# Roots moved from GpSimd to VectorE, and the links of the norm chains spread over more slots

## The chip, the cores and the metric

The kernel runs on one core of one Trainium2 chip. The number that counts is the device time of one execution in microseconds, as a median over runs. Before the change it is 1972.41 us (three runs, 1971.65 to 1972.62).

## What is computed

Two transformer blocks on 256 tokens of width 2048, in fp32, with weights read once from HBM. Cut to what matters here:

```python
# block 1
h = rms_norm(x, norm1_g);  proj = h @ w_in          # 2048 x 6160
qb = rms_norm(qb.reshape(B, S, 8, 128), q_norm_g)   # queries and keys, a norm a head
kb = rms_norm(kb.reshape(B, S, 8, 128), k_norm_g)
out_a = gla_mixer(...)                              # its heads end in rms_norm(o) * silu(r)
out_b = dilated_mixer(qb, kb, vb, rel_bias)
x = x + concat(out_a, out_b) @ w_out
h2 = rms_norm(x, norm2_g)
x = x + (silu(h2 @ w_gate) * (h2 @ w_up)) @ w_down
# block 2, even layer: retention (heads end in rms_norm_nogain(o) * silu(g)) beside a convolution
x = x + even_mixer(rms_norm_2(x, ev_norm_w), ...)
# block 2, odd layer: 32 query heads and 4 key heads of 64
q, k, v, gate = split(rms_norm_2(x, od_norm_w) @ w_in)
q = rope(rms_norm_2(q.reshape(b, s, 32, 64), q_norm_w), pos)
k = rope(rms_norm_2(k.reshape(b, s, 4, 64), k_norm_w), pos)
x = x + (swa_sinks(q, k, v, sinks) * silu(gate)) @ w_out
```

Each `rms_norm` needs one reciprocal square root a row and head: a "root".

## The kernel before

**Products.** Every large product is cut into blocks of 512 output columns, and each block into units of two 128-row slices of weights (eight units where the sum is over 2048). A weight tile comes by DMA into `raw`; ScalarE rounds it to `wh` and VectorE writes the rest, `wl = raw - wh`. This pair is called a cut. A unit on TensorE (`mul`) is then 12 matmuls of 128x512: `wh*xh`, `wl*xh`, `wh*xl` for two slices and two halves of the tokens. There are three buffers of `wh` and `wl` (`NS`), so the cut of unit u+2 waits until unit u-1 is done, and is made while unit u runs.

**The order.** `Plan.lay` writes one list, `plan.order`, and every engine walks the same list and issues its own part of each entry, strictly in that order. For each unit u it says `cut u+2`, then `mul u` first half, then one `step`, then `mul u` second half. A `step` lets each of three lanes (`att`, `fin`, `post`) go on to its next `yield`. So a lane has one slot a unit, in the middle of it. When a block's last unit is said, `launch("post", after(b))` first drains the lane (runs what is left of the former block's work at once, without a slot between), and then says the first entry of the new one. Each norm chain of the queries and keys lives in `post`, and the blocks it runs beside are of eight units, so it has eight slots before it is drained.

**A chain.** For queries and keys of block 1: `qk_evac` (ScalarE, PSUM to `W0`, which is the first half of `TW`, and the square into `W1`, the second half), `qk_sum` (VectorE), the root, `qk_norm` (VectorE multiplies `W0`), and two `qk_turn` (TensorE transposes, ScalarE copies out). The odd layer has `ok_evac` or `oq_evac`, `on_sum`, the root, `on_norm`, `on_rope` twice (six VectorE operations each; the second waits for the first), for the keys also `ok_dup` (four copies), then two turns, which wait for the last `on_rope` (of the keys, for `ok_dup`).

**The root before.** GpSimd runs `root`: 14 small operations on a tile of 128 x 2, 8 or 16 (`st`), each waiting for the one before. Between the first and the second VectorE does one shift, `halve`, which follows its sum at once and waits until GpSimd has made the mean. The same list entry (`qk_sum`, `on_sum`, `g_sum`, `r_sum`, `norm`) holds the sum, the shift and the root. Entries that use the result (`qk_norm`, `on_norm`, `g_n`, `r_n`, and `evacuate` by `rr` for `norm`) wait for `s_root`. There are 21 roots: four of the residual stream, four of block 1's queries and keys, four of GLA heads, four of retention heads, five of the odd layer.

**Other places.** The heads of the odd layer run in lane `att`; `afin` (VectorE, three operations) finishes four of them, and `mix M5` (TensorE transposes of `AW`) follows in lane `fin` after two yields. After the last half of an output block, `add` (VectorE) adds it to `x`, `sq` (ScalarE) squares it for the next norm, and two `xturn` (TensorE transposes of `x`) make the next activations.

Of the kernel before, what the change touches and what calls it, by code (L numbers as in the profile page):

```python
# [7 lines left out]
S, D = 256, 2048  # L8
# [104 lines left out]
class Plan:  # L113
# [78 lines left out]
    def after(self, b):  # L192
        say, kind, a = self.say, b.done[0], b.done[1:]
        if kind == "add":
# [3 lines left out]
            if final and stage < 4:  # L198
                say("sq", stage, j)
                yield  # L200
                for h in range(2):
                    say("xturn", f"X{stage}", 4 * j + 2 * h)
                    yield
                if j == 3:
                    say("norm", stage)
            elif final:
                say("out", j)
        elif kind == "qk":
            key, j = a
# [66 lines left out]
        elif kind == "cg":  # L276
            j = a[0]
            say("cg", j, b.i)
            yield
            yield  # L280
            for h in range(2):
                say("cg_turn", j, h)
                yield
                say("cmix", "M4", 8 + 4 * j + 2 * h, j, h)
                yield
        elif kind == "okv":
            say("ok_evac", b.i)
            yield
            yield from self.od_norm("k")
            say("ok_dup")  # L290
            yield
            yield
            for k in range(2):
                say("ok_turn", k)
                yield
        elif kind == "oq":
            say("oq_evac", a[0], b.i)
            yield
            yield from self.od_norm(a[0])
            yield  # L300
            yield
            for k in range(2):
                say("oq_turn", a[0], k)
                yield
        else:
            assert kind == "og"
            say("og", a[0], b.i)
            yield
            self.lanes["att"].append(self.od_heads(a[0]))

    def od_norm(self, x):
        self.say("on_sum", x)
        yield
        yield
        self.say("on_norm", x)
        yield
        self.say("on_rope", x, 0)
        yield
        self.say("on_rope", x, 1)
# [48 lines left out]
    def finish(self, a, g):  # L368
        self.say("afin", a, g)
        yield  # L370
        yield
        if a == "d":
            self.say("mix", "M0", 8 + 2 * g, "d", g)
        else:
            self.say("mix", "M5", 2 * g, "o", g)
        yield

    def gla(self):
# [24 lines left out]
        for n in range(6):  # L403
# [4 lines left out]
            if n >= 2:  # L408
                say("g_n", n - 2)
# [6 lines left out]
    def retention(self):  # L416
        say = self.say
        for h in range(4):
# [6 lines left out]
            yield  # L425
            yield
# [31 lines left out]
def program(nc, t, out):  # L458
# [50 lines left out]
    for p in plan.order:  # L509
# [9 lines left out]
        if p[0] in ("g_o", "r_pv"):  # L519
# [3 lines left out]
                                            ("norm", "qk_sum", "g_sum", "r_sum", "on_sum"))}  # L523
# [7 lines left out]
    with ctx:  # L531
# [41 lines left out]
        s_root_v, s_root_y, s_root = sem("s_root_v"), sem("s_root_y"), sem("s_root")  # L573
# [405 lines left out]
        def scalar(e):  # L979
# [16 lines left out]
            for p in plan.order:  # L996
# [48 lines left out]
                elif kind == "qk_evac":  # L1045
# [8 lines left out]
                    on.wait_ge(*taken(b))  # L1054
# [128 lines left out]
                elif kind in ("ok_evac", "oq_evac"):  # L1183
# [3 lines left out]
                    if kind == "ok_evac":  # L1187
                        on.wait_ge(s_cg, 2)
                        width = 256
                    else:  # L1190
                        on.wait_ge(s_dup, 2)
                        if a[0]:
                            on.wait_ge(*full("oq_turn", a[0] - 1, 1))
                        width = 512
                    evacuate(T3, b)
                    on.wait_ge(*taken(b))
                    on.wait_ge(s_rope, ropes[("eq_rope", "k", 1, 1)] if kind == "ok_evac" else
                               ropes[("on_rope", a[0] - 1 if a[0] else "k", 1)])
# [20 lines left out]
        def vector(e):  # L1219
# [16 lines left out]
            def halve(p, n):  # L1236

                on.wait_ge(s_root_v, roots[p])
                ts1(ry_[:, 0:n].bitcast(i32), rv_[:, 0:n].bitcast(i32), 1,
                    ALU.logical_shift_right).then_inc(s_root_y, 1)  # L1240

            for p in plan.order:
# [25 lines left out]
                elif kind == "norm":  # L1268
# [4 lines left out]
                    halve(p, 2)  # L1273
# [8 lines left out]
                elif kind == "qk_sum":  # L1282
# [5 lines left out]
                    halve(p, 8)  # L1288
                elif kind == "qk_norm":
                    v = W0.rearrange("p (g d) -> p g d", d=128)  # L1290
                    on.wait_ge(s_root, roots[("qk_sum",) + a])
# [141 lines left out]
                elif kind == "g_sum":  # L1433
# [4 lines left out]
                    halve(p, 2)  # L1438
                elif kind == "g_n":
                    m = a[0]  # L1440
                    k, h2 = gparts[m]
                    on.wait_ge(s_root, roots[("g_sum", m)])
# [45 lines left out]
                elif kind == "r_sum":  # L1488
# [5 lines left out]
                    halve(p, 2)  # L1494
                elif kind == "r_n":
                    h = a[0]
                    on.wait_ge(s_root, roots[("r_sum", h)])
# [47 lines left out]
                elif kind == "on_sum":  # L1545
# [9 lines left out]
                    halve(p, 2 * n)  # L1555
                elif kind == "on_norm":
                    n = 4 if a[0] == "k" else 8
                    on.wait_ge(s_root, roots[("on_sum",) + a])
# [14 lines left out]
        def gpsimd(e):  # L1573
            on = Once(e)
            steps = Steps(s_pool_step)
            done = (s_root, 0)

            def root(p, dst, src, n, width, from_, dst_free=()):

                v, y, q = rv_[:, 0:n], ry_[:, 0:n], rq_[:, 0:n]  # L1580
                yi = y.bitcast(i32)
                on.wait_ge(*from_)
                if roots[p] > 1:
                    on.wait_ge(s_root, roots[p] - 1)
                e.tensor_scalar(v, src, 1.0 / width, 1e-6, ALU.mult, ALU.add).then_inc(s_root_v, 1)  # L1585
                on.wait_ge(s_root_y, roots[p])
                on.wait_ge(*steps.mark(e.tensor_scalar(yi, yi, -1.0, 1597463007.0, ALU.mult, ALU.add)))
                for i in range(3):
                    on.wait_ge(*steps.mark(e.tensor_tensor(q, y, y, ALU.mult)))  # L1589
                    on.wait_ge(*steps.mark(e.tensor_tensor(q, q, v, ALU.mult)))  # L1590
                    on.wait_ge(*steps.mark(e.tensor_scalar(q, q, -0.5, 1.5, ALU.mult, ALU.add)))
                    if i < 2:
                        on.wait_ge(*steps.mark(e.tensor_tensor(y, q, y, ALU.mult)))
                for sem_n in dst_free:
                    on.wait_ge(*sem_n)
                e.tensor_tensor(dst, q, y, ALU.mult).then_inc(s_root, 1)

            for p in plan.order:
                kind, a = p[0], p[1:]
                if kind == "norm":  # L1600
                    free = []
                    if a[0]:
                        was = [taken(b.i) for b in blocks if b.acts == f"X{a[0] - 1}"]
                        for s in (s_read_act, s_read_dve):
                            n = [v for z, v in was if z is s]
                            if n:
                                free.append((s, max(n)))
                    if a[0] == 1:
                        free.append(full(*find("gates")))
                    root(p, rr, nsum, 2, D, (s_nsum, a[0] + 1), free)  # L1610
                elif kind == "qk_sum":
                    root(p, rs[:, 0:8], rs[:, 0:8], 8, 128, (s_qk_sum, nth(*p)))
                elif kind == "g_sum":
                    root(p, rg[a[0]], rg[a[0]], 2, 256, (s_g_sum, nth(*p)))
                elif kind == "r_sum":
                    root(p, rsa, rsa, 2, 256, (s_r_sum, nth(*p)))
                elif kind == "on_sum":
                    n = 8 if a[0] == "k" else 16
                    root(p, rs[:, 0:n], rs[:, 0:n], n, 64, (s_on_sum, nth(*p)))
                elif kind == "bias":  # L1620
# [158 lines left out]
```

## Time and profile before

| | |
|---|---|
| profiled execution | 1971.09 us, span 1969.3 us, granted TensorE clock 1.00 |
| median of the runs | 1972.41 us |
| TensorE busy | 1946.4 us of the span (99%), 9062 matmuls |
| VectorE, ScalarE, GpSimd busy | 1095.9, 939.1, 108.5 us |
| DMA | 178 GB/s read from HBM over the span |

TensorE is busy nearly all the time, and matmuls overlap: a 128x512 matmul is shown as 0.39 us long while the next starts 0.23 us after it. So a wait of TensorE reads some 0.16 us shorter in the list of waits than the time it costs between two starts. What another engine does matters only where TensorE waits for it.

### The profile page before, as it was taken

How to read it: one execution, taken by the hardware profiler on the slowest of the kernel's cores; microseconds unless marked ns; L12 is line 12 of the kernel's file. 1: busy time of each engine (PE TensorE's matmuls, PEld its weight loads, DVE VectorE, ACT ScalarE, POOL GpSimd, SP SyncE). 2: the span in 40 equal slices, each digit the busy share in tenths (PEclk: the TensorE clock that was granted, in tenths of full speed). 3: DMA queues.
4: the chain of work that ended last, by engine and by line, in shares of the span. 5: the costliest groups of instructions: out<-in, count | busy, mean ns of one | idle time of the engine just before them, and what ended most of it. 6: DMA issues, size and time to landing. Idle time of an engine off the chain costs nothing.

```text
span 1969.3 us, 22692 instructions
## 1 busy us (share of the span) xinstructions
PE 1946.4 (99%) x9062; PEld 1600.0 (81%) x9062; DVE 1095.9 (56%) x1330; ACT 939.1 (48%) x1230; POOL 108.5 (6%) x326
## 2 busy tenths in 40 slices
PE   8999999999999999999999999999999999999998
PEld 6788887788888888888888888888888888787787
DVE  4556455664545545445445556544655665666674
ACT  6445354554444344443444554444444464655653
POOL 1111000200000000000000010001100003001100
PEclk9999999999999999999999999999999999999999
DMA  7566564466665666665666566665566655544445
GB/s 238 175 193 171 152 173 159 154 179 192 186 192 190 193 193 190 187 189 193 193 190 191 182 193 183 192 193 171 168 184 189 192 179 176 150 150 141 138 149 161
DMA packets 182441, 352.74 MB, mean 179 GB/s; under 512 B 11136, under 2 KB 11952, under 8 KB 182336
## 3 DMA queue, kind: packets, MB, share of 16 engines
q1 hardware_dynamic: 181520, 349.18, 58.3%
q0 software_dynamic: 816, 2.11, 0.7%
q8 instruction: 71, 1.16, 0.2%
q14 instruction: 34, 0.28, 0.0%
HBM read 349.14 MB, written 2.11 MB: 178 GB/s over the span
## 4 chain that ended last, share of the span: by engine, by line
PE 93%; DVE 3%; POOL 1%; ACT 1%; issue 1%; DMA 0%; DVEq 0%; SPq 0%; ACTq 0%
PE g L790 29%; PE g L792 29%; PE g L791 29%; PE m L755 3%; DVE wl L1225 1%; ACT TW L985 1%; DVE st L1234 1%; PE m L871 1%; DVE TW L1225 1%; ACT wh L988 0%; POOL st L1589 0%; PE ob L889 0%; PE ob L888 0%; PE ob L887 0%; PE m L862 0%
## 5 line engine op out<-in xcount | busy, mean ns | idle before, releaser
L1225 DVE TENSOR_TENSOR wl<-raw,wh 128x1024 fp32r<-128x1024 f32 x657 | 801.5, 1222 | 770.7 <-ACT wh L988 770.1
L988 ACT ACTIVATE wh<-raw 128x1024 fp32r<-128x1024 f32 x657 | 694.5, 1058 | 837.6 <-PE g L792 834.9
L790 PE MATMUL g<-wh,xh 128*128 128x512 f32 x1888 | 748.0, 396 | 2.7 <-DVE wl L1225 2.7
L792 PE MATMUL g<-wh,xl 128*128 128x512 f32 x1888 | 736.8, 390 | 0.0
L791 PE MATMUL g<-wl,xh 128*128 128x512 f32 x1888 | 735.7, 390 | 0.0
L790 PEld LDWEIGHTS g<-wh,xh 128*128 128x128 f32 x1888 | 354.8, 188 | 80.1 <-issue 5.5
L792 PEld LDWEIGHTS g<-wh,xl 128*128 128x128 f32 x1888 | 354.6, 188 | 75.2
L791 PEld LDWEIGHTS g<-wl,xh 128*128 128x128 f32 x1888 | 355.1, 188 | 70.4
L790 PE MATMUL g<-wh,mh 128*128 128x512 f32 x736 | 291.5, 396 | 0.0
L792 PE MATMUL g<-wh,ml 128*128 128x512 f32 x736 | 287.1, 390 | 0.0
L791 PE MATMUL g<-wl,mh 128*128 128x512 f32 x736 | 286.7, 390 | 0.0
L790 PEld LDWEIGHTS g<-wh,mh 128*128 128x128 f32 x736 | 138.2, 188 | 31.2 <-issue 3.9
L792 PEld LDWEIGHTS g<-wh,ml 128*128 128x128 f32 x736 | 138.1, 188 | 29.4
L791 PEld LDWEIGHTS g<-wl,mh 128*128 128x128 f32 x736 | 138.3, 188 | 27.3
L1585 POOL TENSOR_SCALAR st<-st 128x2 f32<-128x2 f32 (+2 forms) x21 | 4.1, 194 | 1632.0 <-DVE st L1234 1631.7
L1225 DVE TENSOR_TENSOR x<-g,x 128x512 f32<-128x512 f32 x72 | 46.4, 685 | 20.0 <-PE g L792 20.0
L985 ACT ACTIVATE A<-g,st 128x512 f32<-128x512 f32 x50 | 31.7, 684 | 31.5 <-PE g L792 31.5
L1091 ACT ACTIVATE PB<-PB,st 128x128 f32<-128x128 f32 x80 | 35.6, 446 | 8.4 <-DVE st L1231 8.4
L988 ACT ACTIVATE xh<-m,small 128x256 fp32r<-128x256 f32 x64 | 26.8, 470 | 20.0 <-PE m L755 20.0
L1228 DVE SCALAR_TENSOR_TENSOR xl<-m,small,xh 128x256 fp32r<-128x256 f32 x64 | 28.0, 479 | 14.4 <-ACT xh L988 14.4
L988 ACT ACTIVATE mh<-m 128x512 fp32r<-128x512 f32 x38 | 22.7, 597 | 26.9 <-PE m L755 26.9
L985 ACT ACTIVATE TW<-g,st 128x512 f32<-128x512 f32 x34 | 21.5, 684 | 24.0 <-PE g L792 19.2
(131 smaller groups left out, 840.4 us busy)
## 6 DMA issues: line engine op xcount, KB each, us to landing
raw<-in_ev_w_in SPq DMA_DIRECT2D x128, 512.0 KB, 3.7
raw<-in_w_in SPq DMA_DIRECT2D x96, 512.0 KB, 3.9
raw<-in_w_gate SPq DMA_DIRECT2D x88, 512.0 KB, 4.3
raw<-in_w_up SPq DMA_DIRECT2D x88, 512.0 KB, 3.7
raw<-in_w_down SPq DMA_DIRECT2D x88, 512.0 KB, 4.7
raw<-in_od_w_in SPq DMA_DIRECT2D x72, 512.0 KB, 3.6
raw<-in_w_out SPq DMA_DIRECT2D x32, 512.0 KB, 4.3
raw<-in_ev_w_out SPq DMA_DIRECT2D x32, 512.0 KB, 3.7
```

The source lines that it names most:

```text
L755: last = e.transpose(dst(c), src(c), ident)
L790: e.matmul(o, hi[:, kt, c], h, start=first, stop=False)
L791: e.matmul(o, hi[:, kt, c], l, start=False, stop=False)
L792: last = e.matmul(o, lo[:, kt, c], h, start=False, stop=end)
L871: last = e.transpose(o[:, 128 * c:128 * c + 128], L[:, 128 * c:128 * c + 128], ident)
L985: return e.activation(o, i, func, scale=scale, bias=bias)
L988: return e.activation(o, i, AF.Copy, scale=scale)
L1091: last = e.activation(L[:, lo:hi], L[:, lo:hi], AF.Exp, bias=mx[:, h, kb:kb + 1], accum_out=sm[:, h, kb:kb + 1])
L1225: return e.tensor_tensor(o, a, b, op)
L1228: return e.scalar_tensor_tensor(out=o, in0=a, scalar=s, in1=b, op0=op0, op1=op1)
L1234: return e.tensor_reduce(o, i, AX, op, negate=negate)
L1585: e.tensor_scalar(v, src, 1.0 / width, 1e-6, ALU.mult, ALU.add).then_inc(s_root_v, 1)
```

## The change

All of `root` moves to VectorE. The helper `halve` and GpSimd's `root` are gone; the root is 12 VectorE operations, and an entry of the list by itself (`qk_root`, `on_root`, `g_root`, `r_root`; for `norm` it stays in the entry). The square of a chain becomes an entry too (`qk_sq`, `on_sq`). The generators say the links with two yields between them instead of one or two. `mix M5` comes two yields later, `sq` goes behind the two `xturn` instead of ahead of them, and `norm` two yields later.

```diff
             if final and stage < 4:
-                say("sq", stage, j)
-                yield
                 for h in range(2):
                     say("xturn", f"X{stage}", 4 * j + 2 * h)
                     yield
+                say("sq", stage, j)
                 if j == 3:
+                    yield
+                    yield
                     say("norm", stage)
...
             say("qk_evac", key, j, b.i)
-            yield
-            say("qk_sum", key, j)
-            yield
-            yield
-            say("qk_norm", key, j)
-            yield
+            for p in ("qk_sq", "qk_sum", "qk_root", "qk_norm"):
+                yield
+                yield
+                say(p, key, j)
             yield
             for k in range(2):
                 say("qk_turn", key, j, k)
...
     def od_norm(self, x):
-        self.say("on_sum", x)
-        yield
-        yield
-        self.say("on_norm", x)
-        yield
-        self.say("on_rope", x, 0)
-        yield
-        self.say("on_rope", x, 1)
+        for p in ("on_sq", "on_sum", "on_root", "on_norm"):
+            yield
+            yield
+            self.say(p, x)
+        for k in range(2):
+            yield
+            self.say("on_rope", x, k)
...
         else:
+            yield
+            yield
             self.say("mix", "M5", 2 * g, "o", g)
...
+            def root(dst, src, n, width, from_, dst_free=()):
+                v, y, q = rv_[:, 0:n], ry_[:, 0:n], rq_[:, 0:n]
+                yi = y.bitcast(i32)
+                on.wait_ge(*from_)
+                on.wait_ge(*steps.mark(e.tensor_scalar(v, src, 1.0 / width, 1e-6, ALU.mult, ALU.add)))
+                on.wait_ge(*steps.mark(ts1(yi, v.bitcast(i32), 1, ALU.logical_shift_right)))
+                on.wait_ge(*steps.mark(e.tensor_scalar(yi, yi, -1.0, 1597463007.0, ALU.mult, ALU.add)))
+                for i in range(3):
+                    on.wait_ge(*steps.mark(stt(q, v, -0.5, y, ALU.mult, ALU.mult)))
+                    on.wait_ge(*steps.mark(tt(q, q, y, ALU.mult)))
+                    if i < 2:
+                        on.wait_ge(*steps.mark(stt(y, q, 1.5, y, ALU.add, ALU.mult)))
+                for sem_n in dst_free:
+                    on.wait_ge(*sem_n)
+                stt(dst, q, 1.5, y, ALU.add, ALU.mult).then_inc(s_root, 1)
```

Three places of the order, before and then after. In these rows `TW<-TW,st` is the norm's product, `TW<-TW,A` and the `TW<-TW` behind it are one `on_rope`, `wl<-raw,wh` is VectorE's part of a cut, and `st<-st` are the small operations of a root.

VectorE, from the sum to the last rope of the odd layer's first queries, before:

```order
L1234 TENSOR_REDUCE st<-TW 128x16
L1231 TENSOR_SCALAR st<-st 128x16
L1225 TENSOR_TENSOR wl<-raw,wh 128x1024 x2
L1225 TENSOR_TENSOR TW<-TW,st 128x512 x2
L1225 TENSOR_TENSOR wl<-raw,wh 128x1024
L1225 TENSOR_TENSOR TW<-TW,A 128x256 x4
L1225 TENSOR_TENSOR TW<-TW 128x8x32 x2
L1225 TENSOR_TENSOR wl<-raw,wh 128x1024
L1225 TENSOR_TENSOR TW<-TW,A 128x256 x4
L1225 TENSOR_TENSOR TW<-TW 128x8x32 x2
```

and after, from the root's last operation on:

```order
L1237 SCALAR_TENSOR_TENSOR st<-st 128x16
L1234 TENSOR_TENSOR wl<-raw,wh 128x1024 x2
L1234 TENSOR_TENSOR TW<-TW,st 128x512 x2
L1234 TENSOR_TENSOR TW<-TW,A 128x256 x4
L1234 TENSOR_TENSOR TW<-TW 128x8x32 x2
L1234 TENSOR_TENSOR TW<-TW,A 128x256 x4
L1234 TENSOR_TENSOR TW<-TW 128x8x32 x2
L1234 TENSOR_TENSOR wl<-raw,wh 128x1024 x3
```

The norm and the two ropes, which had a cut between each, now follow each other with none, and the norm has moved from the third of the block's eight slots to the last. In the list the norm stands in the middle of the block's last unit, and the ropes, the turns and the next evacuation directly behind that unit.

VectorE, where the GLA heads end (`A<-AW,st,A` and `A<-A,st` are `g_n`, `st<-A` is `g_sum`), before:

```order
L1225 TENSOR_TENSOR wl<-raw,wh 128x1024
L1234 TENSOR_REDUCE st<-A 128x2
L1231 TENSOR_SCALAR st<-st 128x2
L1228 SCALAR_TENSOR_TENSOR A<-AW,st,A 128x256 x2
L1225 TENSOR_TENSOR wl<-raw,wh 128x1024
L1234 TENSOR_REDUCE st<-A 128x2
L1231 TENSOR_SCALAR st<-st 128x2
L1228 SCALAR_TENSOR_TENSOR A<-A,st 128x256 x2
```

and after, one cut to the next:

```order
L1234 TENSOR_TENSOR wl<-raw,wh 128x1024
L1243 TENSOR_REDUCE st<-A 128x2
L1250 TENSOR_SCALAR st<-st 128x2
L1240 TENSOR_SCALAR st<-st 128x2
L1252 TENSOR_SCALAR st<-st 128x2
L1237 SCALAR_TENSOR_TENSOR st<-st 128x2
L1234 TENSOR_TENSOR st<-st 128x2
L1237 SCALAR_TENSOR_TENSOR st<-st 128x2 x2
L1234 TENSOR_TENSOR st<-st 128x2
L1237 SCALAR_TENSOR_TENSOR st<-st 128x2 x2
L1234 TENSOR_TENSOR st<-st 128x2
L1237 SCALAR_TENSOR_TENSOR st<-st 128x2
```

Where one shift stood, twelve operations stand between two cuts, and four such roots come in four slots that follow each other.

VectorE, behind an output block of block 1 (`x<-g,x` is `add`, `xl<-m,small,xh` the low half of an `xturn`), before:

```order
L1225 TENSOR_TENSOR x<-g,x 128x512 x2
L1225 TENSOR_TENSOR wl<-raw,wh 128x1024 x2
L1228 SCALAR_TENSOR_TENSOR xl<-m,small,xh 128x256 x2
L1225 TENSOR_TENSOR wl<-raw,wh 128x1024
L1228 SCALAR_TENSOR_TENSOR xl<-m,small,xh 128x256 x2
```

and after:

```order
L1234 TENSOR_TENSOR x<-g,x 128x512 x2
L1234 TENSOR_TENSOR wl<-raw,wh 128x1024
L1237 SCALAR_TENSOR_TENSOR xl<-m,small,xh 128x256 x2
L1234 TENSOR_TENSOR wl<-raw,wh 128x1024
L1237 SCALAR_TENSOR_TENSOR xl<-m,small,xh 128x256 x2
```

The first turn of `x` now stands one slot, that is one unit, nearer to the `add` it reads: half a unit of products behind it instead of one and a half.

## Rows read from the trace of the kernel before

**Rows 1.** Waits of TensorE: us in total, times, longest.

```profile
PE m L755 <- DVE AW L1225: 5.0, 3, 1.7
PE m L755 <- DVE TW L1225: 3.8, 5, 1.1
PE g L790 <- DVE wl L1225: 2.7, 4, 1.1
```

**Rows 2.** Timeline of an undisturbed unit: start us, us, engine, line, operation [idle before].

```profile
58.61 0.39 PE L790 MATMUL g<-wh,xh 128*128 128x512 f32 x1
...
58.87 1.06 ACT L988 ACTIVATE wh<-raw 128x1024 fp32r<-128x1024 f32 x1 [1.66 <-PE g L792]
...
59.96 1.23 DVE L1225 TENSOR_TENSOR wl<-raw,wh 128x1024 fp32r<-128x1024 f32 x1 [1.50 <-ACT wh L988]
...
61.33 0.39 PE L790 MATMUL g<-wh,xh 128*128 128x512 f32 x1
```

**Rows 3.** Timeline where the first root of the residual stream is awaited.

```profile
37.88 1.26 ACT L985 ACTIVATE TW<-g,st 128x512 f32<-128x512 f32 x2 [4.43 <-POOL st L1596]
...
42.50 0.50 PE L790 MATMUL g<-wh,xh 128*128 128x512 f32 x1 [1.09 <-DVE wl L1225]
```

**Rows 4.** Timeline of the first queries of block 1, norm and turn.

```profile
49.54 1.22 DVE L1225 TENSOR_TENSOR TW<-TW,st 128x1024 f32<-128x1024 f32 x1 [3.21 <-POOL st L1596]
...
50.82 0.66 PE L755 MATMUL m<-small,TW 128*128 128x128 f32 x4 [1.15 <-DVE TW L1225]
```

**Rows 5.** Timeline of the odd layer's first queries: norm, first rope, turn.

```profile
1671.23 1.29 DVE L1225 TENSOR_TENSOR TW<-TW,st 128x512 f32<-128x512 f32 x2 [3.38 <-POOL st L1596]
...
1673.58 1.42 DVE L1225 TENSOR_TENSOR TW<-TW,A 128x256 f32<-128x256 f32 x4
1675.03 0.76 DVE L1225 TENSOR_TENSOR TW<-TW 128x256 f32<-128x256 f32 x2
...
1679.12 0.65 PE L755 MATMUL m<-small,TW 128*128 128x128 f32 x4 [0.47 <-DVE TW L1225]
```

**Rows 6.** Timeline of finished heads, first of three such places.

```profile
1722.24 0.68 DVE L1225 TENSOR_TENSOR AW<-ob,st 128x512 f32<-128x512 f32 x1
...
1723.77 0.66 PE L755 MATMUL m<-small,AW 128*128 128x128 f32 x4 [1.66 <-DVE AW L1225]
```

**Rows 7.** Timeline of the odd layer's keys: norm, first rope, copies.

```profile
1647.44 0.76 DVE L1225 TENSOR_TENSOR TW<-TW,st 128x256 f32<-128x256 f32 x2 [2.92 <-POOL st L1596]
...
1649.25 0.89 DVE L1225 TENSOR_TENSOR TW<-TW,A 128x128 f32<-128x128 f32 x4
1650.17 0.49 DVE L1225 TENSOR_TENSOR TW<-TW 128x128 f32<-128x128 f32 x2
...
1653.17 0.90 DVE L1569 COPY A<-TW 128x256 f32<-128x256 f32 x4
```

**Rows 8.** Small operations of VectorE, by shape: busy us, mean ns | idle before.

```profile
L1231 DVE TENSOR_SCALAR st<-st 128x2 f32<-128x2 f32 x32 | 7.3, 229 | 1.1
...
L1225 DVE TENSOR_TENSOR st<-st 128x8 f32<-128x8 f32 x8 | 1.3, 164 | 0.0
```

**Rows 9.** Timeline behind an output block: next unit's first matmul, and the add.

```profile
375.44 0.39 PE L790 MATMUL g<-wh,mh 128*128 128x512 f32 x1
375.64 1.29 DVE L1225 TENSOR_TENSOR x<-g,x 128x512 f32<-128x512 f32 x2 [0.34 <-PE g L792]
```

**Rows 10.** Timeline of VectorE where the last GLA heads end.

```profile
357.02 0.68 DVE L1234 TENSOR_REDUCE st<-A 128x2 f32<-128x512 f32 x1
...
358.73 0.88 DVE L1228 SCALAR_TENSOR_TENSOR A<-A,st 128x256 f32<-128x256 f32 x2
```

**Rows 11.** Two matmuls near the start (timeline), and a window of the end.

```profile
10.20 0.63 PE L790 MATMUL g<-wh,xh 128*128 128x512 f32 x1
10.63 0.63 PE L791 MATMUL g<-wl,xh 128*128 128x512 f32 x1
...
1964.00:1969.00 5.00, 0.17 (x1) 0.00 (x0) 1.29 (x2) 0.00 (x0) 0.00 (x0) 0.84 0.30 105
```

More of the change, by code:

```diff
@@ L402, in gla @@
             yield
-        for n in range(6):
+        for n in range(7):
             if n < 4:
@@ L407, in gla @@
                 say("g_sum", n - 1)
-            if n >= 2:
-                say("g_n", n - 2)
+            if 2 <= n < 6:
+                say("g_root", n - 2)
+            if n >= 3:
+                say("g_n", n - 3)
             yield
@@ L425, in retention @@
             yield
+            say("r_root", h)
             yield
@@ L1053, in scalar @@
                     evacuate(T3, b)
-                    on.wait_ge(*taken(b))
+                elif kind == "qk_sq":
+                    key, j = a
+                    n = nth(*p)
+                    on.wait_ge(*taken(find("qk_evac", key, j)[-1]))
                     if n > 1:
@@ L1272, in vector @@
                     reduce(nsum, ss, ALU.add).then_inc(s_nsum, 1)
-                    halve(p, 2)
+                    free = []
+                    if a[0]:
+                        was = [taken(b.i) for b in blocks if b.acts == f"X{a[0] - 1}"]
+                        for s in (s_read_act, s_read_dve):
+                            n = [v for z, v in was if z is s]
+                            if n:
+                                free.append((s, max(n)))
+                    if a[0] == 1:
+                        free.append(full(*find("gates")))
+                    root(rr, nsum, 2, D, (s_nsum, a[0] + 1), free)
                 elif kind == "add":
@@ L1287, in vector @@
                     reduce(rs[:, 0:8], W1.rearrange("p (g d) -> p g d", d=128), ALU.add).then_inc(s_qk_sum, 1)
-                    halve(p, 8)
+                elif kind == "qk_root":
+                    root(rs[:, 0:8], rs[:, 0:8], 8, 128, (s_qk_sum, nth(*p)))
                 elif kind == "qk_norm":
                     v = W0.rearrange("p (g d) -> p g d", d=128)
-                    on.wait_ge(s_root, roots[("qk_sum",) + a])
+                    on.wait_ge(s_root, roots[("qk_root",) + a])
                     tt(v, v, rs[:, 0:8].unsqueeze(2).to_broadcast([128, 8, 128]), ALU.mult).then_inc(s_qk_norm, 1)
@@ L1437, in vector @@
                            ALU.add).then_inc(s_g_sum, 1)
-                    halve(p, 2)
+                elif kind == "g_root":
+                    m = a[0]
+                    root(rg[m], rg[m], 2, 256, (s_g_sum, m + 1))
                 elif kind == "g_n":
@@ L1441, in vector @@
                     k, h2 = gparts[m]
[L1442 removed]
+                    on.wait_ge(s_root, roots[("g_root", m)])
                     on.wait_ge(*taken(bi[("sr", 1)]))
@@ L1493, in vector @@
                     reduce(rsa, AW[:, 512:1024].rearrange("p (g d) -> p g d", d=256), ALU.add).then_inc(s_r_sum, 1)
-                    halve(p, 2)
+                elif kind == "r_root":
+                    root(rsa, rsa, 2, 256, (s_r_sum, a[0] + 1))
                 elif kind == "r_n":
                     h = a[0]
-                    on.wait_ge(s_root, roots[("r_sum", h)])
+                    on.wait_ge(s_root, roots[("r_root", h)])
                     on.wait_ge(*taken(bi[("gret", 1)]))
@@ L1554, in vector @@
                            ALU.add).then_inc(s_on_sum, 1)
-                    halve(p, 2 * n)
+                elif kind == "on_root":
+                    n = 8 if a[0] == "k" else 16
+                    root(rs[:, 0:n], rs[:, 0:n], n, 64, (s_on_sum, nth(*p)))
                 elif kind == "on_norm":
                     n = 4 if a[0] == "k" else 8
-                    on.wait_ge(s_root, roots[("on_sum",) + a])
+                    on.wait_ge(s_root, roots[("on_root",) + a])
                     norm_n = []
@@ L1575, in gpsimd @@
             steps = Steps(s_pool_step)
[L1576 to L1596, printed above, removed]
@@ L1598, in gpsimd @@
             for p in plan.order:
                 kind, a = p[0], p[1:]
[L1600 to L1620, printed above, removed]
+                if kind == "bias":
```

27 lines of the change are left out of this document (13 added, 14 removed).

## The prediction
> **What bounds the kernel now.** First the busy times: TensorE is the only engine near its limit, so a change of time must be a change in its work or its waits. Its work stays: the same products and transposes. So I read the list of its waits next [rows 1]: 5.0 us in three waits for finished heads (`AW`), 3.8 us in five for a chain's product (`TW`), 2.7 us in four for a cut. Each costs 0.16 us more than listed, since a matmul is shown 0.39 us long and the next starts after 0.23. The chain of waits behind each then shows the root: `qk_norm` and `on_norm` wait on VectorE for GpSimd's last operation for 3 us and more [rows 4, 5, 7], and cuts queue behind the waiting instruction.
>
> The measure for all that follows is an undisturbed unit [rows 2]. TensorE starts it at 58.61 and the next at 61.33: 2.72 us. ScalarE starts the cut for two units later at 58.87, because that is when the unit before is done, and VectorE's `wl` runs from 59.96 to 61.19, that is 1.35 to 2.58 us after the unit's start. What stands behind this `wl` on VectorE starts 2.5 us after the unit's start, however long VectorE was idle before. And `wl` is wanted 5.44 us after it: 2.85 us of cover.
>
> **What goes.** TensorE's stalls at the chains, counted between starts. The cut behind the first root: the evacuation waits on ScalarE 4.43 us for GpSimd, the cut behind it is late [rows 3]; a root on VectorE ends some 2 us sooner, so the 1.09+0.16 = 1.25 us go. Block 1's four chains: one wait of 1.15 [rows 4] and, of the same list, three of 0.72 (3.8 less 1.15 and 0.47, by three); with 0.16 each 3.9 us. The odd layer's first queries: 0.47 for the turn [rows 5] and two late cuts that make up, with 1.09 here and 0.63 at the start, the 2.7 of the list, so 0.97; with three times 0.16 1.9 us. The heads: 5.0+0.48 = 5.5 us; `afin` needs 1.4 us from 1722.24 on [rows 6], and two units more (5.4 us) with no root to wait for in front cover it. Together 12.6 us.
>
> **What comes.** The lane has eight slots a block, and the new chain needs ten or more. So its tail is drained at the block's end: the norm gets the last slot, and the turns (in the odd layer the ropes too) are said directly behind the block's last unit. This norm stands on VectorE behind the last unit's own `wl`, so it cannot start before 2.5 us of that unit, while TensorE is through at 2.72 and then wants the turn. More slots were put between the early links; between the last ones there is less than before.
>
> Block 1's chains: 2.5 + 1.22 [rows 4] + 0.05 = 3.75, less 2.72: 1.0 us, four times 4.1 us. That is what they lost before (3.9): no gain.
>
> The odd layer's keys: norm 0.7 [rows 7], then two ropes. One takes from 1649.25 to 1650.66, 1.41, and the second waits for the first; then the copies, 0.9. 2.5+0.7+2.85+0.9 = 6.95, less 2.72: 4.25 us. Before, these stood in five slots and cost nothing.
>
> The queries, four times: norm 1.25, two ropes of 2.2 (1673.58 to 1675.79) [rows 5]: 2.5+1.25+4.45+0.05 = 8.2, less 2.72: 5.5 us each, 22 in all. For the last three, heads are finished and a root made two units before, and VectorE comes some 0.2 to 0.4 us late to the norm: +0.5 in sum, an estimate. 22.5 us. A bound from below: were the norm ready beforehand, two ropes alone would stand behind the unit, 4.4 us each, 17.6; from above 6.2 each, 25, if the backlog were twice as long. I take 22.5, since the order leaves no way to start sooner.
>
> The turns of `x`: the next unit starts at 375.44, `add` ends at 376.93 [rows 9], 1.49 later. The first turn is now behind half a unit, 1.36. With 0.05 for the signal 0.18 us, and 0.2 with the slower first transpose, in four blocks of three stages: 2.4 us. From below 0, if the first of the two adds were enough, which the wait excludes; from above 0.3 each, 3.6.
>
> The roots on VectorE: the trace has no such root. Small operations of its kind take 0.164 (two tensors) to 0.229 (scalar from a tile) [rows 8], and a dependent one starts some 0.05 after the end of the one before, as the turn behind the norm does [rows 4]. 12 of them: 2.6 to 3.3 us; I take 2.75, as half of them are of the cheaper kinds. Alone in a slot that is under the cover of 2.85, so 17 of the 21 cost nothing (at 3.3 some would cost 0.45 each, up to 6 us in all). The four of the GLA heads follow each other. In the two plain units behind the last head's product VectorE owes 1.2+0.68+2.75+0.88 = 5.5 us [rows 10] and then, without a sum, 4.8, against 2.72: its lag grows from about 0.5 (an estimate) to 3.3 and 5.4. Over the cover that is 0.45, and 2.5 of which 0.45 is already waited and 0.5 is a turn of TensorE: 1.9 us in all. At 3.3 a root it is 3.5, at 2 it is nothing.
>
> The Trainium skill ("VectorE: DVE Perf Modes", section on the TRN2 errata) puts the fixed term of a VectorE operation at about 150 cycles, 0.16 us at its clock, and says (section on the DRAIN) that a semaphore between two costs nothing. Estimated by that page a root is 1.9 us, the term of the GLA heads nothing, and the sum 1.9 us less. The rows of 0.164 agree with its fixed term.
>
> The clock. Matmuls near the start come 0.43 apart, which is 1.2 GHz, against 0.23 later, and in the last 5 us, of which TensorE works 0.17, the granted clock is 0.84 on average [rows 11]: at half for the last 1.6, so it fell to the lower level after TensorE had been idle for some 3 us. Waits of 2 us in the middle show no fall. The five new ones of 4.25 to 5.7 us are longer than the stretch at the end. What a fall costs: at the start seven products came 0.2 late, 1.4 us. None of the five falling costs 0, all five with twice the seven 14. I take three of five, 4.2 us.
>
> The Trainium skill ("TensorE: Matmul & The Clock Gate", Part 1) says that the gate halves the clock when TensorE has been idle, on a beat of its own that the program does not set, and lifts it again only by activity. By that rule some of the five fall and others do not, and which may differ from run to run; the rows of the start and the end agree.
>
> **The sum.** 4.1+4.25+22.5+2.4+1.9+4.2 = 39.4 come, 12.6 go: +26.8 us. On the profiled execution of 1971.1 that is 1997.9; the median of the runs shown is 1.3 above that execution, so I say 1999.
>
> **The rivals.**
> The clock stays up through all waits: 1971.1+22.6 = 1994; falls in each, with more than 1.4 us: 2003. For the second: all five are longer than the idle time at the end. For the first: there the engine stayed idle, here work returns. These are the sides of the forecast, inside its range.
>
> The chains do what the title says, and the time falls: if VectorE reached norm and ropes while TensorE still works on the block's last units, all 12.6 would go and only 2.4 and 1.9 come: 1963. It decides at one point, whether norm and ropes can run ahead of the last unit's `wl`. For it: VectorE is idle over a third of the time, 1.50 us in [rows 2] alone. Against it: VectorE takes the list in order, and the `wl` before it cannot start before the unit before is done.
>
> Only the norms are late: if a turn did not have to wait for the ropes, the five waits of the odd layer would be 2.5+1.25-2.72 = 1.05 us each, 5.2, and the sum 4.1+5.2+2.4+1.9-12.6 = +1.0: 1972, no change. For it: before, the ropes of block 2's odd layer stand in no wait of over 0.5 us. Against: the turns wait for the last rope by its semaphore, and before they had two units of products in front of them.
>
> VectorE becomes the bound: at 3.3 us a root 17 of them run over the cover and the GLA heads lose 3.5 us, which adds 6+1.6 us: 2006. For it: nothing in the trace shows a root on VectorE. Against: half of its operations are of the kind that takes 0.164.
>
> **Chances.** Chains bunched at the block's end, the forecast with both sides of the clock, 0.80, own range 1989 to 2006; VectorE as the bound 0.08; chains free, faster, 0.07; only the norms late 0.05, of which 0.03 within 0.2% and the rest slower. Bounds of the terms: -5 and +2.5 on the queries, -4.2 and +7 (a few us over 1.4 in some) on the clock, -1.9 and +7 on roots; not all at once. The range 1986 to 2008 leaves out the two cases under it and little above. 0.2% is 4 us, about what a measurement of this kernel can tell from no change. Faster by more than that 0.07, within 0.03, slower 0.90.
>
> **What would show it.** In the list of waits, `TW` should stand for some 30 us in nine waits: four near 0.9, one near 4, four near 5.5. `AW` gone. `x<-g,x` new with 12 waits below 0.2 each. GpSimd's root gone; a root of 12 operations on VectorE of 2.6 to 3.3 us. `wl` at the GLA heads, two waits. The granted clock below 1.00 after some of the long waits. Wrong would be: no wait of over 2 us in the odd layer, or `TW<-TW,A` before the last `wl` of its block.

## The result, and the profile after

The changed kernel takes 2001.42 us (median of four runs, 1999.98 to 2002.62) against 1972.03 for the kernel before in the same session (1971.58 to 1972.62): ratio 1.0148, 95% interval 1.0137 to 1.0160. It is 29.4 us slower; 1999 was forecast. The execution that was profiled took 2002.62, with a span of 2000.8 us, 31.5 above the 1969.3 of before.

The busy times answer first (page of the changed kernel: engine, busy us, share, instructions):

```profile
PE 1959.3 (98%) x9062; PEld 1608.7 (80%) x9062; DVE 1134.5 (57%) x1561; ACT 936.5 (47%) x1230; POOL 14.3 (1%) x32
```

The number of matmuls is the same as before, 9062, but they are busy for 12.9 us more: the first hint that some ran at a lower clock. GpSimd's root is gone, and VectorE with 57% is far from a bound. The rest is waits (list of TensorE's waits: us in total, times, longest):

```profile
PE m L757 <- DVE TW L1234: 24.9, 8, 5.4
...
PE m L757 <- DVE A L1604: 4.1, 1, 4.1
PE g L792 <- DVE wl L1234: 0.7, 1, 0.7
```

Against [rows 1] the finished heads (`AW`) are gone and the late cuts have become one, near the start. The wait for `TW` has grown from 3.8 to 24.9 us, and one for the keys (`A`) of 4.1 is new. Behind one of the four longest stands this (timeline of the odd layer's first queries: start us, us, engine, line, operation, idle before):

```profile
1688.97 1.23 DVE L1234 TENSOR_TENSOR wl<-raw,wh 128x1024 fp32r<-128x1024 f32 x1 [0.69 <-ACT wh L990]
...
1690.11 0.39 PE L794 MATMUL g<-wh,xl 128*128 128x512 f32 x1
1690.11 1.29 DVE L1234 TENSOR_TENSOR TW<-TW,st 128x512 f32<-128x512 f32 x2
1691.32 1.42 DVE L1234 TENSOR_TENSOR TW<-TW,A 128x256 f32<-128x256 f32 x4
...
1693.57 1.43 DVE L1234 TENSOR_TENSOR TW<-TW,A 128x256 f32<-128x256 f32 x4
1695.03 0.76 DVE L1234 TENSOR_TENSOR TW<-TW 128x256 f32<-128x256 f32 x2
...
1695.84 1.97 PE L757 MATMUL m<-small,TW 128*128 128x128 f32 x8 [5.34 <-DVE TW L1234]
...
1697.46 0.78 PE L792 MATMUL g<-wh,xh 128*128 128x512 f32 x1
...
1698.04 0.63 PE L793 MATMUL g<-wl,xh 128*128 128x512 f32 x1
...
1698.47 0.63 PE L794 MATMUL g<-wh,xl 128*128 128x512 f32 x1
```

VectorE had been idle for 0.69 us ahead of its `wl`, and still the norm stands behind it, because of the order. TensorE starts its last product when VectorE starts the norm, and everything that follows is serial: norm, rope, rope, then the turn, 5.73 us after that product instead of 0.23. In [rows 5] the same norm and ropes had cuts between them and TensorE had products to go on with. The other three queries of this layer start their turns 5.73 to 5.74 us behind the product before.

The last three rows show the other part of the loss. Products come 0.43 to 0.58 us apart here, as in [rows 11] at the start, and not 0.23. Windows show how long that lasts (window, its length, then PE, PEld, DVE, ACT, POOL busy with their instructions, granted clock, DMA share, GB/s):

```profile
1694.12:1700.94 6.82, 5.10 (x16) 4.42 (x17) 1.99 (x6) 3.29 (x5) 0.00 (x0) 0.50 0.01 2
1758.97:1765.79 6.82, 4.55 (x16) 3.86 (x17) 2.18 (x6) 3.11 (x5) 0.00 (x0) 0.50 0.06 20
1823.82:1830.65 6.83, 3.84 (x13) 3.42 (x14) 2.87 (x8) 2.41 (x3) 0.00 (x0) 0.50 0.14 52
1888.67:1895.50 6.83, 3.48 (x12) 3.09 (x13) 3.20 (x9) 2.05 (x3) 0.00 (x0) 0.50 0.11 39
1666.81:1670.22 3.41, 3.41 (x11) 2.73 (x10) 0.26 (x1) 3.11 (x5) 0.00 (x0) 0.50 0.00 0
```

These are the four blocks of queries and the keys. So all five long waits are followed by TensorE at its lower level, 1.2 GHz, and the clock is 1.00 on either side. At the queries the level fell inside the wait, between 3.6 us (first) and 2.0 us (last) after the last product had ended; behind the keys it fell at 1666.81, when TensorE was already working again for 0.84 us. What a fall costs depends on how much of the low stretch TensorE spends at work: 5.10, 4.55, 3.84, 3.48 and 3.41 us. At half the clock half of that is lost, 1.7 to 2.6 us each and 10.2 us in all, an estimate from these windows.

The same views of the remaining places. Keys, block 1's first chain and the first turn of `x` shown (timeline):

```profile
1661.44 0.39 PE L794 MATMUL g<-wh,xl 128*128 128x512 f32 x1
...
1665.02 0.90 DVE L1604 COPY A<-TW 128x256 f32<-128x256 f32 x4
1665.97 0.86 PEld L757 LDWEIGHTS m<-small,A 128*128 128x128 f32 x8 [4.57 <-DVE A L1604]
```

```profile
58.81 1.22 DVE L1234 TENSOR_TENSOR TW<-TW,st 128x1024 f32<-128x1024 f32 x1
...
60.08 0.98 PE L757 MATMUL m<-small,TW 128*128 128x128 f32 x7 [0.89 <-DVE TW L1234]
```

```profile
387.03 1.29 DVE L1234 TENSOR_TENSOR x<-g,x 128x512 f32<-128x512 f32 x2 [0.34 <-PE g L794]
...
387.97 0.39 PE L794 MATMUL g<-wh,ml 128*128 128x512 f32 x1
...
388.38 0.66 PE L757 MATMUL m<-small,x 128*128 128x128 f32 x4
```

The keys cost 1665.97 - 1661.44 - 0.23 = 4.30 us, a chain of block 1 1.04 (its turn starts at 60.08, 1.27 after the last product at 58.81), and a turn of `x` 0.41 - 0.23 = 0.18. The last is too short to appear in the list of waits, and there are twelve.

A root on VectorE (timeline, the keys' root: first two and last operations):

```profile
1656.00 0.17 DVE L1250 TENSOR_SCALAR st<-st 128x8 f32<-128x8 f32 x1
...
1656.20 0.17 DVE L1240 TENSOR_SCALAR st<-st 128x8 int32<-128x8 int32 x1
...
1658.21 0.17 DVE L1237 SCALAR_TENSOR_TENSOR st<-st 128x8 f32<-128x8 f32 x1
```

From 1656.00 to 1658.38 it is 2.38 us for 12 operations of 0.17, which start 0.20 apart.

### The profile page after: what moved, and what is told of

Its sections match the earlier page's. It is cut to its first block and busy times, and to the rows that moved or that the text cites. A ratio compares the mean times of both kernels' runs of the same rounds, so it can differ in the third digit from the quotient of the medians.

```text
span 2000.8 us, 22608 instructions
## 1 busy us (share of the span) xinstructions
PE 1959.3 (98%) x9062; PEld 1608.7 (80%) x9062; DVE 1134.5 (57%) x1561; ACT 936.5 (47%) x1230; POOL 14.3 (1%) x32
## 5 line engine op out<-in xcount | busy, mean ns | idle before, releaser
L757 PE MATMUL m<-small,TW 128*128 128x128 f32 x112 | 19.3, 319 | 24.9 <-DVE TW L1234 24.9
L990 ACT ACTIVATE A<-m 128x512 f32<-128x512 f32 x28 | 16.6, 598 | 53.8 <-PE m L757 53.8
L757 PEld LDWEIGHTS m<-small,TW 128*128 128x128 f32 x112 | 15.5, 164 | 29.4 <-DVE TW L1234 28.3
```

Source lines behind the costliest of these rows:

```text
L757: last = e.transpose(dst(c), src(c), ident)
L990: return e.activation(o, i, AF.Copy, scale=scale)
```

## The experiments

All medians stand beside the kernel before, measured on the same chip in the same session (1971.9 to 1972.2).

**1. One slot between the odd layer's links.** The change with `od_norm` respaced; the copies of the keys directly behind the last rope.

```diff
         for p in ("on_sq", "on_sum", "on_root", "on_norm"):
             yield
-            yield
             self.say(p, x)
...
             yield from self.od_norm("k")
-            yield
-            yield
             say("ok_dup")
             yield
+            yield
```

> The changed kernel with one yield instead of two between the links of the odd layer's chains, and the keys' copies directly behind the last rope: square, sum, root, norm and both ropes get slots 1 to 6 of the block's eight, the first turn slot 8. Roots stay on VectorE, block 1's chains, the turns of x and the GLA heads stay as changed. Theory (the chain's tail is drained at the block's end, and the wait lowers the clock): the five waits of 4.3 and 5.5 us go (26.3), and with them the five falls of the clock (about 10 us more, worked out from 20.4 us of work at the lower level), so 2001.4 - 36 = 1965, and no granted clock below 1.00 inside the run. Rival (VectorE is loaded too much by roots in the odd layer): the waits only move to the cuts and to the finished heads, and the time stays over 1985.

Measured: 1965.98 us, ratio 0.9968 (0.9956 to 0.9981). It gives back 35.4 us and is faster than both kernels; that is more than the loss of 29.4, since the change had also done away with older waits. Its waits (list of TensorE's waits):

```profile
...
PE m L755 <- DVE TW L1232: 3.5, 4, 0.9
...
```

The four waits for `TW` are block 1's; the five of the odd layer are gone, and the granted clock is 0.999 over the span against 0.992. The roots stayed on VectorE. So the loss is that of the number of slots in the odd layer's chains.

**2. TensorE kept busy in the five waits.** Matmuls whose result is overwritten are put between the last product and the turn: 16 ahead of the wait for the keys, 22 ahead of each wait for queries.

```diff
+            def fill(o, n):
+                for _ in range(n):
+                    e.matmul(o[:, 0:256], ident, C("evcos"), start=True, stop=True)
...
+                        fill(bank(*p), 22)
                         on.wait_ge(s_rope, ropes[("on_rope", a[0], 1)])
```

> The changed kernel with matmuls of constants into the turn's own bank, whose result is overwritten: 16 of 128x256 ahead of the first turn of the odd layer's keys, 22 ahead of the first turn of each of its four query blocks. They need about 0.22 us each, so 3.5 and 4.8 us, and lie inside waits of 4.3 and 5.5 us. Theory (the waits lower the clock, and the products behind them then come 0.43 instead of 0.23 us apart): no granted clock below 1.00 between the start and the end, products 0.23 apart behind each wait, and 8 to 10 us less: 1992. Rival (products behind a wait are slow because cuts or weights come late): same 2001, the slow products stay. A filler that runs too long would cost up to 1 us a wait.

Measured: 2010.54 us, ratio 1.0195 (1.0181 to 1.0209), slower than the changed kernel where faster was expected. The timeline at the first queries says why:

```profile
1690.31 9.66 PE L762 MATMUL m<-small 128*128 128x256 f32 x44
...
1700.59 0.48 PE L796 MATMUL g<-wh,xh 128*128 128x512 f32 x1
1700.91 0.39 PE L797 MATMUL g<-wl,xh 128*128 128x512 f32 x1
```

The 22 fp32 matmuls were issued as 44 instructions of 0.22 us, so the filler outlasted the wait by some 4 us. The clock stayed up (the next product follows after 0.32), but the experiment bounds nothing, since the filler itself is the loss. Halved, it is the next one.

**3. Half the filler.** 8 and 11 matmuls instead of 16 and 22.

> The changed kernel with TensorE kept busy in the five long waits: matmuls whose result is overwritten (8 ahead of the wait of the odd keys, 11 ahead of each of the four of the queries, each issued as two instructions of 0.22 us: 3.5 and 4.8 us, less than the waits of 4.3 and 5.5). Theory: the waits stay as long, but the granted clock no longer falls behind them, which gives back about 2 us at each: about 1991.5 us. Rival: the clock's part was the smaller one, the time stays above 1997; then the 10 us lie elsewhere.

Measured: 1992.64 us, ratio 1.0105 (1.0091 to 1.0119), 8.8 us less than the changed kernel. The first queries (timeline):

```profile
1688.65 0.39 PE L798 MATMUL g<-wh,xl 128*128 128x512 f32 x1
1688.88 4.91 PE L762 MATMUL m<-small 128*128 128x256 f32 x22
1694.40 1.09 PE L757 MATMUL m<-small,TW 128*128 128x128 f32 x8 [0.61 <-DVE TW L1242]
1695.25 0.48 PE L796 MATMUL g<-wh,xh 128*128 128x512 f32 x1
```

```profile
1683.00:1695.00 12.00, 11.39 (x54) 9.46 (x53) 10.18 (x29) 2.12 (x2) 0.00 (x0) 1.00 0.51 155
```

From the last product to the turn it is 5.75 us, as without the filler (5.73): the wait is unchanged. But the granted clock is 1.00 (second fence: window over that wait; 1.000 over the span against 0.992), and the next product starts 0.85 us after the turn instead of 1.62. So the five falls are worth 8.8 us by the medians, 9.4 by the two profiled spans (2000.8 and 1991.4): 1.8 to 1.9 us each on average. One by one, from the last product of a block to that of the next, the changed kernel takes 1.6 us (keys), 2.4, 2.1 and 1.8 us (first three queries) more than this one.

**4. The squares ahead of the turns of x.** The change with this part alone as before (the norm's two slots go with it).

```diff
+                say("sq", stage, j)
+                yield
                 for h in range(2):
                     say("xturn", f"X{stage}", 4 * j + 2 * h)
                     yield
-                say("sq", stage, j)
                 if j == 3:
-                    yield
-                    yield
                     say("norm", stage)
```

> The changed kernel with the square ahead of the two turns of x again, as before the change (the norm then stands where it stood before too). Theory: twelve waits of TensorE for the add, 0.18 us each, go: 2.1 us less, 1999.3; where the clock falls differently in single runs it can be 1.5 us off. Rival (the waits are made good by something late behind them): 2001.4, and other waits of TensorE in the list.

Measured: 1999.40 us, ratio 1.0139 (1.0124 to 1.0155): 2.0 us less, and the twelve short waits are gone from the trace: the first of these turns starts at 389.53, 0.23 behind the product at 389.30, and the others likewise. The two intervals overlap, so it is the trace that shows it more than the times.

**5. Only the roots.** The slots of before, with each root on VectorE straight behind its sum.

```diff
             say("qk_sum", key, j)
+            say("qk_root", key, j)
...
         self.say("on_sum", x)
+        self.say("on_root", x)
```

> The roots on VectorE alone: every root stands directly behind its sum, and all else of the list is in the slots of the kernel before (turns of x, ropes, finished heads, g_n). Theory: the waits for GpSimd's roots go (1.25 at the first root, 3.9 in block 1, most of 1.9 at the first odd queries), while in the odd layer a root of 2.4 us in front of the finishing of heads makes these three waits longer, from 1.82 to about 3.7 each: 1972.0 - 6.5 + 5.7 = 1971. Rival (the move to VectorE itself costs, since its order is full): 1976 or more, with waits at the cuts of the GLA and retention heads.

Measured: 1984.78 us, ratio 1.0062 (1.0049 to 1.0075): slower than before, where I expected no loss. The list of TensorE's waits:

```profile
PE m L759 <- DVE AW L1236: 11.1, 3, 3.7
PE g L794 <- DVE wl L1236: 6.6, 7, 1.3
...
```

Seven late cuts stand where [rows 1] had four, and one of them in block 1 reads so (timeline, VectorE and TensorE):

```profile
65.68 1.21 DVE L1245 TENSOR_REDUCE st<-TW 128x8 f32<-128x1024 f32 x1
...
68.93 0.39 PE L796 MATMUL g<-wh,xl 128*128 128x512 f32 x1
...
69.23 2.35 DVE L1236 TENSOR_TENSOR wl<-raw,wh 128x1024 fp32r<-128x1024 f32 x2
...
70.50 0.50 PE L794 MATMUL g<-wh,xh 128*128 128x512 f32 x1 [1.18 <-DVE wl L1236]
```

Sum and root are one lump of 3.6 us (65.68 to 69.3) in front of a `wl`, more than the 2.85 us of cover that the prediction read from [rows 2]. At the heads the lump stands ahead of `afin`, and the wait of TensorE doubles from 1.7 to 3.7 us; behind these three the clock was at its lower level too (window behind the first):

```profile
1726.92:1730.32 3.40, 3.34 (x10) 2.86 (x11) 2.98 (x7) 0.60 (x1) 0.00 (x0) 0.50 0.73 219
```

Between starts the listed waits are 5.9 us longer than before (heads +6.1, cuts +4.4, `TW` -4.6), of 11.8 in the profiled spans. Three falls of some 2 us each would make up the rest; the next experiment asks that.

The kernel of 9, which has one slot between sum and root, shows one late cut where this one shows seven: with the root on VectorE one slot there helps, and two slots at every link are what does harm.

**6. The same, with the heads' mix two slots later.** Asked whether the clock had a part in the loss of the kernel of 5.

```diff
         else:
+            yield
+            yield
             self.say("mix", "M5", 2 * g, "o", g)
```

> The kernel with only the roots moved (1984.8 us, the slots of before, each root straight behind its sum) and the odd layer's mix two slots later. Theory for why that kernel missed: its three head waits of 3.84 us, behind a root, lowered the granted clock, and with the waits the clock's loss goes: 11.5 us of waits and some 5 us of clock, 1968.5 us. It would still lose the four cuts of 1.3 to 1.5 us behind the roots of block 1. Rival: the clock had no part, only the 11.5 us go: 1973.5.

Measured: 1970.11 us, ratio 0.9991 (0.9982 to 1.0000), between the two answers. The three waits for heads turned into three for the cut behind the root (timeline of the first; VectorE's `wl` and TensorE):

```profile
1724.80 0.39 PE L798 MATMUL g<-wh,xl 128*128 128x512 f32 x1
...
1724.85 1.22 DVE L1238 TENSOR_TENSOR wl<-raw,wh 128x1024 fp32r<-128x1024 f32 x1
...
1726.12 0.50 PE L796 MATMUL g<-wh,xh 128*128 128x512 f32 x1 [0.93 <-DVE wl L1238]
```

That is 1.09 us each between starts, so of 11.5 us 8.2 went. The granted clock is 1.00 at all three places now. The medians differ by 14.7; the 6.5 that are left are the only sign, in times, of the clock's part here (three falls, 2.2 each; in the profiled executions, where the spans differ by 11.9, it is 3.7 in all). The direction is shown, the size of it here is not.

**7. Only the slots.** The list of the changed kernel, with the roots made by GpSimd as before.

> The list of the changed kernel (all its slots, the later mix, the squares behind the turns), with the roots made on GpSimd as before, behind their sums. Theory: the loss belongs to the slots, so all five waits of 4.3 to 5.5 us of the odd layer and the falls of the clock behind them are there, with the first root's 1.25 us of before: 2000 to 2003 us. Rival: the lump of twelve operations on VectorE makes the norms late; without it the time is near the kernel before, 1972 to 1980.

Measured: 2001.84 us, ratio 1.0150 (1.0136 to 1.0164), the time of the changed kernel. Its waits for `TW` and for the keys are the same to 0.1 us (list of TensorE's waits):

```profile
PE m L757 <- DVE TW L1234: 25.0, 8, 5.4
...
PE m L757 <- DVE A L1578: 4.2, 1, 4.2
```

The level of the clock falls at the same five places, too. The engine of the root makes no difference to this loss. One detail: the 1.25 us at the first root [rows 3] didn't come back, with GpSimd's root as with VectorE's in 5.

**8. Only the later mix.** The kernel before, with the edit of 6.

> The kernel before with one edit of the change alone: the odd layer's mix is put two slots later; its roots stay on GpSimd, its slots stay as they were. Theory: the head waits of the kernel before (AW, 5.0 us in 3) go, with the 0.5 us that stood around them, and nothing takes their place: about 1966.5 us against 1972.1 (ratio 0.997). Rival: the waits come back at the next product that needs the same head, 1972.

Measured: 1965.85 us, ratio 0.9969 (0.9957 to 0.9980): 6.0 us faster, and `AW` is gone from its waits, while those for `TW` and `wl` stay near [rows 1]:

```profile
...
PE m L757 <- DVE TW L1227: 3.8, 5, 1.2
PE g L792 <- DVE wl L1227: 3.3, 4, 1.2
```

**9. One slot everywhere.** The edits of 1 and 4, and in block 1's chains one slot between links, too.

```diff
             for p in ("qk_sq", "qk_sum", "qk_root", "qk_norm"):
                 yield
-                yield
                 say(p, key, j)
             yield
+            yield
```

> The changed kernel with one slot instead of two between all links of the chains (block 1's queries and keys as well as the odd ones) and the squares of x ahead of its turns, as before; the roots stay on VectorE and the later mix stays. Theory: against the kernel whose odd chains alone were shortened (1966.0 us) it loses the four waits of 1.04 us in block 1 (4.2) and the twelve of 0.18 us at the turns of x (2.1): about 1959.7. Rival: in block 1 a root of 2.4 us doesn't fit into one slot there, and waits of the size that the kernel with the roots put right behind the sums showed (1.3 to 1.5 us, four times) take the place of the four: about 1965.

Measured: 1958.71 us, ratio 0.9933 (0.9919 to 0.9946), the fastest of all: 13.2 us under the kernel before and 42.7 under the changed one. Beside the load of `x` at the start, one wait of 0.8 us is left in TensorE's list:

```profile
...
PE g L789 <- DVE wl L1231: 0.8, 1, 0.8
```

The odd layer's queries show how (timeline of VectorE):

```profile
1666.95 1.29 DVE L1231 TENSOR_TENSOR TW<-TW,st 128x512 f32<-128x512 f32 x2
1668.16 1.22 DVE L1231 TENSOR_TENSOR wl<-raw,wh 128x1024 fp32r<-128x1024 f32 x1
1669.29 1.43 DVE L1231 TENSOR_TENSOR TW<-TW,A 128x256 f32<-128x256 f32 x4
...
1671.44 1.22 DVE L1231 TENSOR_TENSOR wl<-raw,wh 128x1024 fp32r<-128x1024 f32 x1
```

A cut stands between norm and rope again, and each cut is in time. With one slot a link, the chain fits into the eight slots of a block.

## Why the prediction held, and where its sizes were off

The forecast was slower, 1999 in a range of 1986 to 2008; 2001.42 was measured. The step that decided it, that two slots a link don't fit into a block's eight, so that norm, ropes and turns are said in one piece behind the last unit, is what the trace shows and what experiments 1, 7 and 9 confirm: the slots alone cost it all, and with one slot a link instead of two in the odd layer alone the kernel is faster than before. The rivals in which norms or ropes come out of TensorE's way are answered by the rows from 1690.11 to 1695.84: norm and both ropes stand between the last product and the turn. The terms of the sum, from the trace of the profiled execution, between starts:

| term | predicted us | measured us |
|---|---|---|
| gone: first root, block 1, first queries, heads | 12.6 | 12.6 (none is left in the trace) |
| block 1's four chains | 4.1 | 4 x 1.04 = 4.2 |
| odd layer's keys | 4.25 | 4.30 |
| odd layer's queries | 22.5 | 4 x 5.50 = 22.0 |
| twelve turns of `x` | 2.4 | 12 x 0.18 = 2.1 |
| GLA heads | 1.9 | 0.3 |
| clock behind the long waits | 4.2 | 9.4 (experiment 3) |
| clock at the start | 0 | about 1.4 |
| sum | 26.8 | 31.1, of 31.5 in the spans |

That 1999 came within 2.4 us of 2001.42 is in part luck. The clock and the start are 6.6 us more than was forecast, the GLA heads, the queries and the turns 2.4 less, and the medians differ by 29.4 where the two profiled spans differ by 31.5. The 0.5 us for a late VectorE at the last three queries didn't come: all four turns start 5.73 to 5.74 behind the product.

Of the signs that were named, the nine waits came: four near 0.9, one of 4.1 (under `A`, since its turn waits for the copies) and four of 5.4, 29.0 us in all. `x<-g,x` and `wl` at the GLA heads are not in the list, since these waits are too short for it, and a root is shorter than the 2.6 to 3.3 us that were said. The rival of VectorE as the bound counted 6 us for seventeen roots at 0.45 each, which would be 7.7; at 2.4 us a root it didn't arise.

**The clock.** This is the term that was mis-sized. "Three of five, at 1.4 us" became five of five at 1.8 to 1.9. The rival of the upper side, a fall in each, gave 2003, and the measured time lies between it and the forecast. The price of 1.4 was counted from seven products at the start; here eight transposes and the products behind them run slow, for 3.4 to 5.1 us of work in each low stretch. The mechanism was argued from the idle end of the kernel and is now shown by making TensorE work through the same wait. The Trainium skill ("TensorE: Matmul & The Clock Gate", Part 1) says that the gate halves the clock when TensorE has been idle; the rows agree, the clock being 0.50 behind every wait of 3.8 us and more in the stream of products, in four kernels (the changed one and those of 4, 5 and 7), and 1.00 through the waits of 1.8 us (between starts) at [rows 6]. My reading of the rule, that some waits would get through, did not come true in any of them. No wait between 1.8 and 3.8 us was tried.

**The start.** A difference that no edit explains. Both kernels, from 11.60 to 14.60 (window), first before, then the changed one:

```profile
11.60:14.60 3.00, 3.00 (x17) 2.53 (x16) 1.54 (x2) 1.66 (x3) 0.00 (x0) 1.00 1.05 398
```

```profile
11.60:14.60 3.00, 3.00 (x11) 2.51 (x10) 1.63 (x2) 1.78 (x3) 0.00 (x0) 1.00 1.05 397
```

The changed kernel starts 11 matmuls there and the one before 17, at the same loads: six products of 0.23 us, 1.4 us, for a later rise of the clock. The profile's column puts 1.00 in both, so the lower level is inferred here, as in the prediction, from products that start 0.43 us apart, as they do behind the long waits. The kernel of 4 has the list of the changed one up to there and starts 16 in this window; the kernel of 9 starts 11 and is the fastest. So the list does not set it. It looks like chance of the execution, which one trace a kernel cannot show, and it is no part of what the change does.

**GLA heads.** I took 2.75 us for a root and the trace has 2.38 (2.5 for 16 columns). The backlog that was to build up over four roots then reaches over the cover only once, for 0.26 us (the product at 366.22 starts 0.49 after the one before it). The Trainium skill ("VectorE: DVE Perf Modes", section on the DRAIN) says, of eight copies, that a semaphore after each costs nothing extra; with the fixed term of its section on the TRN2 errata the prediction made 1.9 us of that, an estimate. The operations are 0.17 long, which agrees with the fixed term, but they start 0.20 apart: with a wait on the one before, 0.03 to 0.04 comes on top of each. The measured root lies about halfway between the two estimates.

**What was argued and is now shown in part only.** That the roots cost next to nothing in a slot of their own holds (one late cut of 0.26 in all); what happens without the slot is experiment 5. The 1.25 us of the first root went for a reason that I gave (a quicker root), but they also went in experiment 7 with the slow root, so that a quicker root was not needed. Which of the moved entries does it there was not tried.

**The gain in it.** The rival "chains do what the title says" was put at 1963, with 4.3 us of losses at the turns of `x` and the GLA heads. Without those it is 1958.5 on the profiled execution (1971.1 - 12.6). Experiment 9, which is another list than the change, gained 13.2 us between medians (1958.71 against 1971.89) where 12.6 were priced. The idea was sound; two yields a link were one too many.

## What to carry to other kernels

Count the slots before spacing a chain: links times slots must fit into what the block offers, since what doesn't fit is run in one piece at the block's end, where nothing is left to hide it. A lump of work on an engine that keeps its order does harm like work that comes late: the operations ahead of a cut must stay under the cover of that cut. And price a long wait of TensorE with more than its length, for the slower products behind it: here waits of 4.3 and 5.5 us cost some 2 us more each. Filling the wait with idle matmuls gets those back, but removing the wait gets all.

## What was not expected of the hardware

- The clock fell at all five waits of 4.3 and 5.5 us and all three of 3.8 us, and at none of the three of 1.8 us in the kernel before. How long it stayed low can differ behind like waits: behind the keys 3.4 us in the changed kernel (from 1666.81) and some 6.8 in that of 7 (from 1662.8).
- It can fall after work has come back: at 1666.81, 0.84 us after the first transpose.
- An fp32 matmul with a 128x256 operand was issued as two instructions, 0.22 us each, so that 22 took 9.66 us.
